# Sums of squares as two short passes instead of one full one: retention's variances and the scan's group norms

## The chip, the cores and the metric

The kernel runs on one core of a Trainium2 chip. The metric is the device time of one launch in microseconds. A core has five engines that run side by side and wait for each other through semaphores: TensorE (PE in profiles; PEld is its weight loading), VectorE (DVE), ScalarE (ACT), GpSimd (POOL) and SyncE (SP), which here only starts transfers. Each engine works through its own list in order.

## The reference

A three-part network on 512 positions of width 1024, in fp32: a first block with three mixers, a layer of retention and neighbourhood attention, a layer with a bidirectional state scan (SSD), and a gated feed-forward block behind each of the last two. Two places matter here. Both take a mean of squares over features and scale by its inverse root.

```python
# retention: 8 heads of 64, y already has its head's mean taken off
var = jnp.mean(jnp.square(y - mu), axis=-1, keepdims=True)
y = ((y - mu) * lax.rsqrt(var + EPS)) * ret_gn_g
...
# scan: 4 groups of 512 features
y = y + xh * d_skip                       # then gated by silu(z)
yg = y.reshape(bsz, s, SSD_GROUPS, SSD_INNER // SSD_GROUPS)
yg = yg * lax.rsqrt(jnp.mean(yg * yg, axis=-1, keepdims=True) + EPS)
```

## The kernel before

Activations lie with features on the 128 partitions and the 512 positions along the row; a tile is 128 x 512. Weights come in slots of 128 x 1024 through a ring of five buffers.

**Short and full products.** A weight matmul is done as three short products (type fp32r): ScalarE copies the operand to fp32r, the high part (`hi`); VectorE subtracts it from the operand, the low part (`lo`); TensorE adds high x high, high x low and low x high (L439 to L441). Matmuls with plain fp32 operands are full products; the trace shows each as two records. Sums over features are full products with a matrix of ones: `ones64` (ones within each head of 64) for retention, `ones` for the scan.

**Retention.** Four pairs of heads, p = 0 to 3, eight steps r = 2p, 2p+1. TensorE's list alternates scores, states and values of a pair with the tiles of `in2`. The sum of squares of pair p-1 (`ret_variance`) stands behind the tiles of step 2p; the last one stands in `out2_pe`, in front of the second k of `out2`'s lead (n == 1). Around it: VectorE copies y out of PSUM (`keep_ret`, L1390), ScalarE squares it (`square`, L1193), TensorE sums (L1073), ScalarE takes Ln and Exp (`roots`), VectorE refines and scales (`norm`).

**The scan.** Four groups g, each of eight heads and four output tiles. Per group the order in TensorE's list (`ssd_pe`) is: states and between-chunk products, mixed with tiles of `z`; then for i = 0 to 3 a set of four transposes that carry y into PSUM (`carried`, L2514) and the head products (`inside`, L2521). `carried(g, 0)` waits for `comb`, which VectorE's `carry(g, 2)` completes (L2799); `inside(g, i)` waits for `mlu`, the weighed matrices of heads 2i, 2i+1 (`weigh`, L2836). For the last group, out3's first products stand between them and wait for `ylo`, y's low parts (`low`, L2885).

The decay matrices of the heads come in pairs: SP loads two rows of `cum_rows` for each head (`load_rows`), and waits for the head two before to have been moved; ScalarE moves one to PSUM (`moved_back`, L2652), VectorE joins (`join`, L2826), ScalarE exponentiates (`decays`, L2662), VectorE weighs. In group g ScalarE's list runs: `squares(g-1, 2)`, moves of heads 0, 1, a weight split, `squares(g-1, 3)`, `decays(g, 0, 1)`, `moved_back(g, 2, 3)`, a weight split, `decays(g, 2, 3)`, and so on.

The sum of squares of group g-1 is spread over the engines. ScalarE squares the four tiles (L2626), GpSimd adds them up in three adds (L2759), TensorE sums over features (`norm_sum`, L2530; for the last group in `out3_lead_pe`, L2602). GpSimd's list in group g is written out by hand:

```python
        for g in range(SG):
            if g:
                pool.wait_ge(comb, 6 * g + 1)
                add_squares(pool, g - 1, 1)
                gate(pool, g - 1, 3)
                add_squares(pool, g - 1, 2)
            for d, (c, held) in enumerate(((2, 3), (1, 0))):
                pool.wait_ge(comb, 6 * g + 2 + d + 1)
                nc.gpsimd.tensor_tensor(y12[:, c, :], y12[:, c, :], y12[:, held, :], ALU.add).then_inc(y12_added, 1)
            if g:
                add_squares(pool, g - 1, 3)
```

`comb` 6g+3 and 6g+4 come from VectorE's `carry(g, 1)`. `norm_sum(g-1)` stands in front of `carried(g, 0)`, in the last group in front of `carried(g, 1)`; it waits for all three adds (`yadd`). Squares and sums are held in the rows of `xbc` that B and C of the group no longer need (`B_TILE + g`, `C_TILE + g`).

Of the kernel before, what the change touches and what calls it, by code (L numbers as in the profile page):

```python
# [185 lines left out]
def build(nc, dr, ctx, start):  # L186
# [110 lines left out]
    sq_2 = at("sq_2", [P, KT, S], ST + 64)  # L297
    nrm_2 = at("nrm_2", [P, 3, S], ST + 58)
    sq_u = at("sq_u", [P, KT, S], ST + 72)
    nrm_u = [at(f"nrm_u{i}", [P, S], ST + kb)[:, :] for i, kb in enumerate((96, 100, 98))]  # L300
    sq_x = at("sq_x", [P, KT, S], ST + 32)
    nrm_x = [at(f"nrm_x{i}", [P, S], ST + kb)[:, :] for i, kb in enumerate((88, 93, 90))]
# [573 lines left out]
    sign = nstat[:, 3, 0:1]  # L876
    rg, rh = sem("rg"), sem("rh")
    rz, ra, rv, ryc = sem("rz"), sem("ra"), sem("rv"), sem("ryc")
    g_sq, g_var, g_ln, g_norm, g_gate, g_last = (sem(n) for n in ("g_sq", "g_var", "g_ln", "g_norm", "g_gate", "g_last"))
    bt_load, bm_done, cm_load = [sem("bt_load0"), sem("bt_load1")], sem("bm_done"), sem("cm_load")  # L880
    (nvp, nvc, nz, ns, nmax, nexp, nrec, nnorm, ntp, ntc, ny, nyc) = (
        sem(n) for n in ("nvp", "nvc", "nz", "ns", "nmax", "nexp", "nrec", "nnorm", "ntp", "ntc", "ny", "nyc"))
# [186 lines left out]
        mm.then_inc(rv, 1)  # L1069

    def ret_variance(pe, p):
        pe.wait_ge(g_sq, p + 1)
        nc.tensor.matmul(bank[2 + p % 2][:, :], C["ones64"], gsq[:, :], start=True, stop=True).then_inc(g_var, 1)  # L1073

    def two_pe(pe):
        before, home = SUMS["in2"]
# [42 lines left out]
    def out2_pe(pe):  # L1119
        for n, k in enumerate(MIX2_ORDER):  # L1120
            pe.wait_ge(mixlo, KT + n + 1)
            if n == 1:
                ret_variance(pe, PAIRS - 1)
            for t in range(LEAD["out2"]):
                if n == 0:
                    bank_clear(pe, "out2", t)
                    pe.wait_ge(lo_done, last_slot("out2", t) + 1 + HEAD)
                mm = three("out2", t, k, a_hi, a_lo, S, n == KT - 1, MIX2_ORDER[0])
                if n == KT - 1:
                    mm.then_inc(slot_done, 1)  # L1130
# [136 lines left out]
    def two_dve(dve):  # L1267
# [183 lines left out]
        for r in range(RET_STEPS):  # L1451
            p, half = r // 2, r % 2
            if half:
                states(p)
                if p:
                    norm(p - 1)
            else:
                if p:
                    keep_ret(p - 1)
                weigh(p)  # L1460
                query_decay(p)
            if r < RET_STEPS - 1:
                for t in RET_TILES[r]:
                    tile(t)
# [1 line left out]
        take(27)  # L1466
        lo_to(dve, split_ahead("in2", 27))
        keep_ret(PAIRS - 1)
        for n in range(1, 4):
            low(n)  # L1470
        low(4)
        low(5)
        norm(PAIRS - 1)
# [728 lines left out]

    def one_pool(pool):
        pool.wait_ge(cst_load, 16)
        nc.gpsimd.tensor_copy(tri_r[:, 0, :], C["neg_tri"])
        nc.gpsimd.tensor_copy(tri_r[:, 1, :], C["neg_ones"]).then_inc(tri_ready, 1)
        tile_gone(pool, "in1", 1)
# [35 lines left out]
                mask(aw, n, a_done, ZU * p + n + 1, am_done)  # L2243


    (dtw_load, dtw_hi, dtw_lo, dtp, dtc, cump, cum_x, dt_ok, tri_load, y12_added, cs_rows) = (
        sem(n) for n in ("dtw_load", "dtw_hi", "dtw_lo", "dtp", "dtc", "cump", "cum_x", "dt_ok", "tri_load", "y12_added", "cs_rows"))
    xmid, xtap, xsilu, zs_done = sem("xmid"), sem("xtap"), sem("xsilu"), sem("zs_done")
    (tbp, tbc, gp, gl_done, txp, xtc, vt_done, stp, hub, hu, inter, comb) = (
        sem(n) for n in ("tbp", "tbc", "gp", "gl_done", "txp", "xtc", "vt_done", "stp", "hub", "hu", "inter", "comb"))  # L2250
# [50 lines left out]

    def cum_pe(pe):
        pe.wait_ge(dt_ok, 1)
        pe.wait_ge(tri_load, 16)
        tile_gone(pe, "xbc", 8)
        for half, (mf, mb) in enumerate((("gt", "lt"), ("le", "ge"))):
            out = bank[CUM_BANK][:, 256 * half:256 * (half + 1)].rearrange("p (c d h) -> p c d h", c=TT, d=2)
            nc.tensor.matmul(out[:, :, 0, :], M[mf], da[:, :, 0, :], start=True, stop=True)
            nc.tensor.matmul(out[:, :, 1, :], M[mb], da[:, :, 1, :], start=True, stop=True)
        nc.tensor.matmul(bank[TOTAL_BANK][:, 0:256], C["ones"], flat(da), start=True, stop=True).then_inc(cump, 1)  # L2310
        for c in range(TT):
            for d, m in enumerate(("le", "ge")):
                mm = nc.tensor.matmul(bank[CST_BANK][SH * d:SH * (d + 1), c * P:(c + 1) * P], da[:, c, d, :], M[m], start=True, stop=True)
        mm.then_inc(cump, 1)
# [51 lines left out]
    def cum_act(act):  # L2366
# [2 lines left out]
            nc.scalar.activation(flat(dst), source, ACT.Exp).then_inc(cum_x, 1)  # L2369
        nc.scalar.activation(flat(lndt), flat(lndt), ACT.Ln).then_inc(cum_x, 1)  # L2370
        act.wait_ge(cump, 2)
        act.wait_ge(tri_load, 16)
# [73 lines left out]
    def ssd_pe(pe):  # L2446
# [78 lines left out]
            mm.then_inc(intra, 1)  # L2525

        def norm_sum(g):
            pe.wait_ge(yadd, 3 * (g + 1))
            pe.wait_ge(hu, 4 * min(g + 2, SG))
            nc.tensor.matmul(bank[6][:, :], C["ones"], xbc[:, B_TILE + g, :], start=True, stop=True).then_inc(ysum, 1)  # L2530

        for t in range(2):
            for q in range(4):
# [10 lines left out]
        for g in range(SG):  # L2544
# [17 lines left out]
            for i in range(4):  # L2562
                first, second = (4 * g + 4 + i // 2, 2 * (i % 2)), (4 * g + 4 + i // 2, 2 * (i % 2) + 1)
                if i == 0 and not last:
                    part_z(*first)
                    part_z(*second)
                if g and i == last:
                    norm_sum(g - 1)
                carried(g, i)
                if i:  # L2570
# [15 lines left out]
    def out3_step(pe, t, k):  # L2586
# [6 lines left out]
        if k % 8 == 7:  # L2593
            mm.then_inc(slot_done, 1)

    def out3_lead_pe(pe):
        pe.wait_ge(joined, HEADS)
        for t in (2, 3):
            for k in range(8):
                out3_step(pe, t, k)  # L2600
        pe.wait_ge(yadd, 3 * SG)
        nc.tensor.matmul(bank[6][:, :], C["ones"], xbc[:, B_TILE + SG - 1, :], start=True, stop=True).then_inc(ysum, 1)  # L2602
        for t in range(4):
            for k in range(8, 12):
                out3_step(pe, t, k)
        for t in range(4):
            for k in range(12, XS_TILES):
                out3_step(pe, t, k)
        pe.wait_ge(yev, XS_TILES)
        for t in range(4, FULL["out3"]):  # L2610
            tile_pe(pe, "out3", t, y_hi, y_lo)
        out_tail_pe(pe, 2, y_hi, y_lo, sq_b, nrm_b[:, 0, :])
# [8 lines left out]
    def squares(g, i):  # L2621
# [3 lines left out]
            act_.wait_ge(yadd, 3 * g + 1)  # L2625
        nc.scalar.activation(square_home(g, i), xbc[:, k, :], ACT.Square).then_inc(ysq, 1)  # L2626

    def group_roots_act(g):
        act_.wait_ge(ysum, g + 1)
        nc.scalar.activation(xbc[:, C_TILE + g, :], bank[6][:, :], ACT.Ln, scale=1.0 / GW, bias=eps_col[:, :]).then_inc(yln, 1)  # L2630
        act_.wait_ge(yln, 2 * g + 1)
# [6 lines left out]
    def ssd_act(act):  # L2638
# [33 lines left out]
        for g in range(SG):  # L2672
# [18 lines left out]
            if g:  # L2691
                squares(g - 1, 3)
            decays(g, 0, 1)
            moved_back(g, 2, 3)
            hi_to(act, z0 + 4 * g + 7)
            decays(g, 2, 3)
# [64 lines left out]
    def ssd_dve(dve):  # L2761
# [76 lines left out]
        def evac_y(g, i):  # L2838
# [2 lines left out]
            nc.vector.scalar_tensor_tensor(out=xbc[:, k, :], in0=xbc[:, k, :], scalar=pcol("d_skip", k), in1=bank[2 + i % 2][:, :],  # L2841
                                           op0=ALU.mult, op1=ALU.add).then_inc(yev, 1)

        def root_first(g):
            dve.wait_ge(yln, 2 * g + 2)
# [43 lines left out]
        for g in range(SG):  # L2889
# [27 lines left out]
            else:  # L2917
                lo_to(dve, z0 + 4 * g + 5)
                carry(g, 2)
                weigh(g, 0, 1)  # L2920
            if last:
                low(0)
                low(1)
# [53 lines left out]
        lo_to(dve, z0 + 4 * SG + 4)  # L2977
        for k in range(9, 12):
            low(k)
        lo_to(dve, z0 + 4 * SG + 7)  # L2980
        group_roots(SG - 1)
        for i in range(4):
# [83 lines left out]
    def _(act):  # L3066
# [28 lines left out]
        up_act(act, 0)  # L3095
        nc.scalar.preload_act_table_set(LOGEXP)
        act.wait_ge(glo, FT)
        act.dma_start(wdt[:, :, :], dr["w_dt"]).then_inc(dtw_load, 16)
        act.wait_ge(dtw_load, 16)
# [3 lines left out]
        act.dma_start(tri[:, :, :], dr["tri"]).then_inc(tri_load, 16)  # L3103
        hi_to(act, PLAN["xbc"]["slot0"] + 5)
        xbc_act(act)
        turned_x(act, 0, 2)
# [201 lines left out]
```

## Time and profile before

| | |
|---|---|
| median of 3 executions | 1658.52 us (1658.38 to 1660.28) |
| profiled execution | 1660.08 us, its span 1658.3 us |
| TensorE busy | 1643.7 us, 99% of the span |
| VectorE, ScalarE, GpSimd busy | 1160.1, 797.2, 210.7 us |

The span runs from the first to the last instruction. Times in a timeline are microseconds from its start; a matmul's end is modelled, so the distance between starts tells more of TensorE than a duration. The scan takes from about 1035 to 1205 us, retention from about 370 to 482 us. Idle time is shown in brackets with what ended it.

### The profile page before, as it was taken

To read this page: it belongs to the slowest core of one execution; us is meant where nothing else is said; L and a number is where in the kernel's file an instruction comes from. 1 tells how busy PE (TensorE), PEld (TensorE's weight loads), DVE (VectorE), ACT (ScalarE), POOL (GpSimd) and SP (SyncE) were. 2 spreads that over 40 slices of the span, in tenths; PEclk is the share of its full clock that TensorE was granted. 3 is DMA by queue.
4 is the path that set the end of the run, shared out by engine and by line. 5 is a ranking of instruction groups with operands and counts; after the bars stand their busy time and mean duration, and the time that the engine had idled before them with its cause. 6 is when DMAs were issued, how large, how long until landed. Compare 5 with 4: busy or idle time off the path is not lost.

```text
span 1658.3 us, 21247 instructions
## 1 busy us (share of the span) xinstructions
PE 1643.7 (99%) x8278; PEld 1335.5 (81%) x8278; DVE 1160.1 (70%) x1681; ACT 797.2 (48%) x1367; POOL 210.7 (13%) x244
## 2 busy tenths in 40 slices
PE   9999999999999999999999999999999999999998
PEld 6877878788888888888888888777688888888887
DVE  5585874985668887664238999799984788666324
ACT  5475753552254554443224455777853554444221
POOL 0442100442110011110000000122200011111000
PEclk9999999999999999999999999999999999999999
DMA  6211223234332232333332224555333223233332
GB/s 236 91 64 63 77 77 126 93 92 86 77 102 69 97 102 91 101 97 103 93 96 83 94 92 123 153 153 149 106 102 112 71 97 102 90 101 94 97 92 73
DMA packets 55108, 166.53 MB, mean 100 GB/s; under 512 B 6816, under 2 KB 10144, under 8 KB 54880
## 3 DMA queue, kind: packets, MB, share of 16 engines
q1 hardware_dynamic: 51024, 158.80, 30.5%
q0 software_dynamic: 1536, 2.10, 1.2%
q10 hardware_dynamic: 2448, 4.27, 0.8%
q8 instruction: 66, 1.08, 0.3%
q14 instruction: 34, 0.28, 0.1%
HBM read 160.82 MB, written 2.23 MB: 98 GB/s over the span
## 4 chain that ended last, share of the span: by engine, by line
PE 91%; DVE 6%; ACT 2%; DMA 1%; issue 1%; ACTq 0%; DVEq 0%; SPq 0%
PE bank L439 25%; PE bank L441 25%; PE bank L440 25%; PE bank L456 2%; PE bank L457 2%; PE bank L458 2%; PE bank L2493 1%; DVE cv L2427 1%; PE bank L2505 1%; PE bank L2521 1%; DVE a_lo L813 1%; DVE w_lo L402 1%; ACT a_hi L776 1%; DVE x L707 1%; PE bank L1619 1%
## 5 line engine op out<-in xcount | busy, mean ns | idle before, releaser
L439 PE MATMUL bank<-a_hi,w_hi 128*128 128x512 f32 x1384 | 556.4, 402 | 2.5 <-DVE a_lo L595 1.8
L402 DVE TENSOR_TENSOR w_lo<-raw,w_hi 128x1024 fp32r<-128x1024 f32 (+1 forms) x257 | 327.5, 1280 | 329.8 <-ACT w_hi L395 329.0
L441 PE MATMUL bank<-a_hi,w_lo 128*128 128x512 f32 x1384 | 539.5, 390 | 0.0
L440 PE MATMUL bank<-a_lo,w_hi 128*128 128x512 f32 x1384 | 538.9, 389 | 0.0
L395 ACT ACTIVATE w_hi<-raw 128x1024 fp32r<-128x1024 f32 (+1 forms) x259 | 267.9, 1041 | 316.4 <-DMA raw<-in_w_down 141.5
L439 PEld LDWEIGHTS bank<-a_hi,w_hi 128*128 128x128 f32 x1384 | 259.9, 188 | 68.0 <-issue 13.2
L440 PEld LDWEIGHTS bank<-a_lo,w_hi 128*128 128x128 f32 x1384 | 260.0, 188 | 59.4 <-issue 7.4
L441 PEld LDWEIGHTS bank<-a_hi,w_lo 128*128 128x128 f32 x1384 | 259.8, 188 | 55.2
L1500 ACT ACTIVATE u<-bank,par 128x512 f32<-128x512 f32 x88 | 68.5, 779 | 176.0 <-DVE bank L864 176.0
L1543 POOL TENSOR_TENSOR gv<-u 128x512 f32<-128x512 f32 x44 | 57.4, 1304 | 577.1 <-DVE u L1519 577.1
L441 PE MATMUL bank<-g_hi,w_lo 128*128 128x512 f32 x308 | 119.8, 389 | 0.0
L439 PE MATMUL bank<-g_hi,w_hi 128*128 128x512 f32 x308 | 119.8, 389 | 0.0
L440 PE MATMUL bank<-g_lo,w_hi 128*128 128x512 f32 x308 | 119.8, 389 | 0.0
L2427 DVE SCALAR_TENSOR_TENSOR cv<-bank,par,cv 128x510 f32<-128x510 f32 (+1 forms) x96 | 71.7, 748 | 2.5
L1519 DVE SCALAR_TENSOR_TENSOR u<-bank,par,u 128x511 f32<-128x511 f32 x88 | 66.0, 750 | 3.1
L439 PEld LDWEIGHTS bank<-g_hi,w_hi 128*128 128x128 f32 x308 | 57.8, 188 | 12.1
L440 PEld LDWEIGHTS bank<-g_lo,w_hi 128*128 128x128 f32 x308 | 57.8, 188 | 12.1
L441 PEld LDWEIGHTS bank<-g_hi,w_lo 128*128 128x128 f32 x308 | 57.8, 188 | 11.9
L1516 DVE SCALAR_TENSOR_TENSOR u<-bank,par,u 128x511 f32<-128x511 f32 x88 | 65.0, 739 | 0.0
L864 DVE TENSOR_TENSOR bank<-bank,nrm_u 128x512 f32<-128x512 f32 x88 | 60.8, 690 | 0.8 <-PE bank L441 0.8
L456 PE MATMUL bank<-a_hi,w_hi 128*128 128x256 f32 (+1 forms) x156 | 49.9, 320 | 2.4 <-DVE a_lo L813 1.2
L2742 POOL TENSOR_TENSOR y<-y 128x512 f32<-128x512 f32 x8 | 10.1, 1287 | 303.6 <-DVE y L2799 303.6
(429 smaller groups left out, 2478.8 us busy)
## 6 DMA issues: line engine op xcount, KB each, us to landing
raw<-in_w_up SPq DMA_DIRECT2D x86, 512.0 KB, 3.6
raw<-in_w_in SPq DMA_DIRECT2D x50, 512.0 KB, 3.7
raw<-in_w_out SPq DMA_DIRECT2D x32, 512.0 KB, 3.7
raw<-in_w_down SPq DMA_DIRECT2D x32, 512.0 KB, 3.5
raw<-in_w_xbc SPq DMA_DIRECT2D x23, 512.0 KB, 3.6
back<-cum_rows SPq DMA_DIRECT2D x32, 256.0 KB, 4.2
em<-cum_rows SPq DMA_DIRECT2D x32, 256.0 KB, 5.3
raw<-in_w_z SPq DMA_DIRECT2D x16, 512.0 KB, 4.5
```

The source lines that it names most:

```text
L395: nc.scalar.activation(hi_of(q)[:, 0:w], raw_of(q)[:, 0:w], ACT.Copy).then_inc(hi_done, 1)
L402: nc.vector.tensor_tensor(lo_of(q)[:, 0:w], raw_of(q)[:, 0:w], hi_of(q)[:, 0:w].bitcast(F32), ALU.subtract).then_inc(lo_done, 1)
L439: nc.tensor.matmul(out, wh, rhs_hi[:, k, :], start=k == first, stop=False)
L440: nc.tensor.matmul(out, wh, rhs_lo[:, k, :], start=False, stop=False)
L441: return nc.tensor.matmul(out, wl, rhs_hi[:, k, :], start=False, stop=stop)
L456: nc.tensor.matmul(out, wh, rhs_hi[:, k, cols], start=start, stop=False, skip_group_check=True)
L864: nc.vector.tensor_tensor(tile_bank(name, t)[:, :], tile_bank(name, t)[:, :], r, ALU.mult).then_inc(scaled, 1)
L1500: nc.scalar.activation(u[:, t % 4, :], tile_bank(name, t)[:, :], ACT.Identity, scale=pcol(f"ffn_w{layer}", 3 * t + 1), bias=pcol(f"ffn_b{l ...
L1516: nc.vector.scalar_tensor_tensor(out=ut[:, 1:S], in0=pt_[:, 0:S - 1], scalar=pcol(w, 3 * t), in1=ut[:, 1:S], op0=ALU.mult, op1=ALU.add).th ...
L1519: nc.vector.scalar_tensor_tensor(out=ut[:, 0:S - 1], in0=pt_[:, 1:S], scalar=pcol(w, 3 * t + 2), in1=ut[:, 0:S - 1], op0=ALU.mult, op1=ALU ...
L1543: nc.gpsimd.tensor_tensor(gv[:, i % 2, :], u[:, 2 * i % 4, :], u[:, 2 * i % 4 + 1, :], ALU.mult).then_inc(prod, 1)
L2427: nc.vector.scalar_tensor_tensor(out=dst, in0=tile_bank("xbc", tile)[:, a + by:b + by], scalar=pcol("conv_w", 5 * tile + tap), in1=dst, op ...
```

## The change

Each of the eight sums becomes two short products with a copy of the ones in fp32r: one over the high part of the squares, one over the low part, added in the same PSUM bank.

- GpSimd makes the fp32r copies of `ones` and `ones64` at the start.
- Retention: ScalarE's `square` gets a second step, the high copy (into `gsq_parts`); VectorE gets `square_low`, behind `query_decay` in steps 2, 4, 6, and for the last pair between `low(2)` and `low(3)`. TensorE waits for `g_low`. The last sum moves from n == 1 to n == 2.
- Scan: ScalarE gets `group_high_act(g-1)` between `decays(g, 0, 1)` and `moved_back(g, 2, 3)`; it waits for the third add. VectorE gets `group_low(g-1)` behind `weigh(g, 0, 1)` (in the last group behind the weight split that follows them). TensorE's sum waits for `sum_low` and moves one i later: in front of `carried(g, 1)` in groups 1 and 2, of `carried(g, 2)` in group 3. For the last sum the two new steps stand behind `high(11)` and `low(11)`, and the products behind the first four of out3's middle steps.
- Two load semaphores are merged into one (`scan_load`).

```diff
@@ buffers
+    ones_r = at("ones_r", [P, P], 103, F32R)
+    ones64_r = at("ones64_r", [P, P], 102, F32R)
+    gsq_parts = at("gsq_parts", [P, 2, S], ST + 76, F32R)
+    xbc_r = at("xbc_r", [P, 24, S], ST + 32, F32R)
@@ ret_variance
-        pe.wait_ge(g_sq, p + 1)
-        nc.tensor.matmul(bank[2 + p % 2][:, :], C["ones64"], gsq[:, :], start=True, stop=True).then_inc(g_var, 1)
+        pe.wait_ge(g_low, p + 1)
+        nc.tensor.matmul(bank[2 + p % 2][:, :], ones64_r[:, :], gsq_parts[:, 0, :], start=True, stop=False)
+        nc.tensor.matmul(bank[2 + p % 2][:, :], ones64_r[:, :], gsq_parts[:, 1, :], start=False, stop=True).then_inc(g_var, 1)
@@ out2_pe
-            if n == 1:
+            if n == 2:
                 ret_variance(pe, PAIRS - 1)
@@ two_act, square
             nc.scalar.activation(gsq[:, :], p2[:, RET_V + p, :], ACT.Square).then_inc(g_sq, 1)
+            act.wait_ge(g_sq, 2 * p + 1)
+            nc.scalar.activation(gsq_parts[:, 0, :], gsq[:, :], ACT.Copy).then_inc(g_sq, 1)
@@ two_dve
+        def square_low(p):
+            dve.wait_ge(g_sq, 2 * p + 2)
+            nc.vector.tensor_tensor(gsq_parts[:, 1, :], gsq[:, :], gsq_parts[:, 0, :].bitcast(F32), ALU.subtract).then_inc(g_low, 1)
...
                 query_decay(p)
+                if p:
+                    square_low(p - 1)
...
-        for n in range(1, 4):
+        for n in range(1, 3):
             low(n)
+        square_low(PAIRS - 1)
+        low(3)
@@ one_pool
+        nc.gpsimd.tensor_copy(ones_r[:, :], C["ones"])
+        nc.gpsimd.tensor_copy(ones64_r[:, :], C["ones64"])
@@ ssd_pe
         def norm_sum(g):
-            pe.wait_ge(yadd, 3 * (g + 1))
             pe.wait_ge(hu, 4 * min(g + 2, SG))
-            nc.tensor.matmul(bank[6][:, :], C["ones"], xbc[:, B_TILE + g, :], start=True, stop=True).then_inc(ysum, 1)
+            group_sum(pe, g)
...
-                if g and i == last:
+                if g and i == 1 + last:
                     norm_sum(g - 1)
@@ new, and out3_lead_pe
+    def group_sum(pe, g):
+        pe.wait_ge(sum_low, g + 1)
+        nc.tensor.matmul(bank[6][:, :], ones_r[:, :], xbc_r[:, C_TILE + g, :], start=True, stop=False)
+        nc.tensor.matmul(bank[6][:, :], ones_r[:, :], xbc_r[:, B_TILE + g, :], start=False, stop=True).then_inc(ysum, 1)
...
-        pe.wait_ge(yadd, 3 * SG)
-        nc.tensor.matmul(bank[6][:, :], C["ones"], xbc[:, B_TILE + SG - 1, :], start=True, stop=True).then_inc(ysum, 1)
         for t in range(4):
             for k in range(8, 12):
                 out3_step(pe, t, k)
+            if t == 0:
+                group_sum(pe, SG - 1)
@@ ssd_act
+    def group_high_act(g):
+        act_.wait_ge(yadd, 3 * (g + 1))
+        nc.scalar.activation(xbc_r[:, C_TILE + g, :], xbc[:, B_TILE + g, :], ACT.Copy).then_inc(yln, 1)
...
             decays(g, 0, 1)
+            if g:
+                group_high_act(g - 1)
             moved_back(g, 2, 3)
...
             high(4 * SG - 8 + i)
+        group_high_act(SG - 1)
@@ ssd_dve
+        def group_low(g):
+            dve.wait_ge(yln, 3 * g + 1)
+            nc.vector.tensor_tensor(xbc_r[:, B_TILE + g, :], xbc[:, B_TILE + g, :], xbc_r[:, C_TILE + g, :].bitcast(F32), ALU.subtract).then_inc(sum_low, 1)
...
                 carry(g, 2)
                 weigh(g, 0, 1)
+            if g:
+                group_low(g - 1)
...
             low(k)
+        group_low(SG - 1)
         lo_to(dve, z0 + 4 * SG + 7)
```

## Rows read from the trace of the kernel before

**Rows 1.** The page, busy time of each engine.
```profile
PE 1643.7 (99%) x8278; PEld 1335.5 (81%) x8278; DVE 1160.1 (70%) x1681; ACT 797.2 (48%) x1367; POOL 210.7 (13%) x244
```

**Rows 2.** The chain, one retention sum: start us, us, what.
```profile
409.26 0.86 PE bank L1073 x2
410.12 0.23 PE bank L439
```

**Rows 3.** Timeline of TensorE behind head products: start us, us, what.
```profile
1118.16 0.50 PE L439 MATMUL bank<-a_hi,w_hi 128*128 128x512 f32 x1
1118.49 0.39 PE L440 MATMUL bank<-a_lo,w_hi 128*128 128x512 f32 x1
```

**Rows 4.** Timeline of ScalarE, retention's first square.
```profile
406.45 0.61 ACT L1193 ACTIVATE gsq<-p 128x512 f32<-128x512 f32 x1
```

**Rows 5.** TensorE's waits, 1040 to 1240 us: total, times, longest.
```profile
PE bank L2514 <- DVE y L2799: 1.3, 1, 1.3
PE bank L2480 <- DVE xtok L2805: 0.3, 1, 0.3
```

**Rows 6.** Windows: PE, PEld, DVE, ACT, POOL busy, granted clock, DMA, GB/s.
```profile
1163.00:1183.00 20.00, 19.99 (x72) 12.89 (x73) 19.88 (x29) 15.56 (x39) 8.54 (x8) 1.00 0.47 111
```

**Rows 7.** Timeline of ScalarE in groups 1 and 3.
```profile
1088.59 2.45 ACT L2662 ACTIVATE em<-em,lbias 128x128 f32<-128x128 f32 x8 [0.63 <-DVE em L2826]
1090.95 2.40 ACT L2652 ACTIVATE bank<-back,between_bias 128x128 f32<-128x128 f32 x8
...
1109.05 2.57 ACT L2652 ACTIVATE bank<-back,between_bias 128x128 f32<-128x128 f32 x8 [3.85 <-DMA em<-cum_rows]
...
1175.12 2.44 ACT L2662 ACTIVATE em<-em,lbias 128x128 f32<-128x128 f32 x8
```

**Rows 8.** Timeline of GpSimd: the third add in groups 1 and 3.
```profile
1095.86 1.27 POOL L2759 TENSOR_TENSOR xbc<-xbc 128x512 f32<-128x512 f32 x1
...
1182.46 1.28 POOL L2759 TENSOR_TENSOR xbc<-xbc 128x512 f32<-128x512 f32 x1
```

**Rows 9.** Timeline of VectorE in groups 1 and 3 and behind them.
```profile
1095.39 1.36 DVE L2826 COPY_PREDICATED em<-later,bank 128x512 f32<-128x512 int32 x2
...
1098.14 1.28 DVE L2799 TENSOR_TENSOR y<-bank,cume 128x512 f32<-128x512 f32 x2
...
1199.14 0.69 DVE L2836 TENSOR_TENSOR em<-em,gmat 128x512 f32<-128x512 f32 x1 [0.22 <-ACT em L2662]
...
1225.07 2.49 DVE L2885 TENSOR_TENSOR y_lo<-xbc,y_hi 128x512 fp32r<-128x512 f32 x4
```

**Rows 10.** Timeline of TensorE in groups 1 and 3 and behind them.
```profile
1100.45 1.02 PE L2530 MATMUL bank<-xbc,cst 128*128 128x512 f32 x2
...
1102.86 0.66 PE L2514 MATMUL bank<-cst,y 128*128 128x128 f32 x4
...
1185.54 0.66 PE L2514 MATMUL bank<-cst,y 128*128 128x128 f32 x4 [1.28 <-DVE y L2799]
...
1187.16 1.12 PE L2530 MATMUL bank<-xbc,cst 128*128 128x512 f32 x2
1188.13 0.60 PE L2514 MATMUL bank<-cst,y 128*128 128x128 f32 x4
1188.48 0.48 PE L439 MATMUL bank<-y_hi,w_hi 128*128 128x512 f32 x1
...
1200.17 1.09 PE L2521 MATMUL bank<-em,xtok 128*64 128x128 f32 x16
...
1226.71 0.39 PE L439 MATMUL bank<-y_hi,w_hi 128*128 128x512 f32 x1
```

**Rows 11.** Timeline of SP's queue: a row load of group 1.
```profile
1103.38 0.43 SPq L2995 DMA_DIRECT2D em<-cum_rows  x1
```

**Rows 12.** The core's span and its mean granted TensorE clock.
```profile
core 0: 1658.3 us, clock 1.000
```

**Rows 13.** Full products at the start: ns min/median/max, first and last start.
```profile
L690 PE MATMUL bank<-spin x8: 592/752/1219, 1.4 to 6.2; 128*128 128x512 f32 x8
```

More of the change, by code:

```diff
@@ L878, in build @@
     rz, ra, rv, ryc = sem("rz"), sem("ra"), sem("rv"), sem("ryc")
-    g_sq, g_var, g_ln, g_norm, g_gate, g_last = (sem(n) for n in ("g_sq", "g_var", "g_ln", "g_norm", "g_gate", "g_last"))
+    g_sq, g_low, g_var, g_ln, g_norm, g_gate, g_last = (sem(n) for n in ("g_sq", "g_low", "g_var", "g_ln", "g_norm", "g_gate", "g_last"))
     bt_load, bm_done, cm_load = [sem("bt_load0"), sem("bt_load1")], sem("bm_done"), sem("cm_load")
@@ L2243, in one_pool @@
                 mask(aw, n, a_done, ZU * p + n + 1, am_done)
-    (dtw_load, dtw_hi, dtw_lo, dtp, dtc, cump, cum_x, dt_ok, tri_load, y12_added, cs_rows) = (
-        sem(n) for n in ("dtw_load", "dtw_hi", "dtw_lo", "dtp", "dtc", "cump", "cum_x", "dt_ok", "tri_load", "y12_added", "cs_rows"))
+    (scan_load, dtw_hi, dtw_lo, dtp, dtc, cump, cum_x, dt_ok, y12_added, cs_rows) = (
+        sem(n) for n in ("scan_load", "dtw_hi", "dtw_lo", "dtp", "dtc", "cump", "cum_x", "dt_ok", "y12_added", "cs_rows"))
     xmid, xtap, xsilu, zs_done = sem("xmid"), sem("xtap"), sem("xsilu"), sem("zs_done")
@@ L2303, in cum_pe @@
         pe.wait_ge(dt_ok, 1)
-        pe.wait_ge(tri_load, 16)
+        pe.wait_ge(scan_load, 32)
         tile_gone(pe, "xbc", 8)
@@ L2371, in cum_act @@
         act.wait_ge(cump, 2)
-        act.wait_ge(tri_load, 16)
+        act.wait_ge(scan_load, 32)
         nc.scalar.activation(later[:, :], M["gt"], ACT.Copy)
@@ L2626, in squares @@
         nc.scalar.activation(square_home(g, i), xbc[:, k, :], ACT.Square).then_inc(ysq, 1)
+    sum_low = sem("sum_low")
+    def group_high_act(g):
+        act_.wait_ge(yadd, 3 * (g + 1))
+        nc.scalar.activation(xbc_r[:, C_TILE + g, :], xbc[:, B_TILE + g, :], ACT.Copy).then_inc(yln, 1)
     def group_roots_act(g):
@@ L2630, in group_roots_act @@
         nc.scalar.activation(xbc[:, C_TILE + g, :], bank[6][:, :], ACT.Ln, scale=1.0 / GW, bias=eps_col[:, :]).then_inc(yln, 1)
-        act_.wait_ge(yln, 2 * g + 1)
+        act_.wait_ge(yln, 3 * g + 2)
         nc.scalar.activation(xbc[:, B_TILE + g, :], xbc[:, C_TILE + g, :], ACT.Exp, scale=-0.5).then_inc(yln, 1)
@@ L2842, in evac_y @@
                                            op0=ALU.mult, op1=ALU.add).then_inc(yev, 1)
+        def group_low(g):
+            dve.wait_ge(yln, 3 * g + 1)
+            nc.vector.tensor_tensor(xbc_r[:, B_TILE + g, :], xbc[:, B_TILE + g, :], xbc_r[:, C_TILE + g, :].bitcast(F32), ALU.subtract).then_inc(sum_low, 1)
         def root_first(g):
[L2845 removed]
+            dve.wait_ge(yln, 3 * g + 3)
             nc.vector.scalar_tensor_tensor(out=xbc[:, C_TILE + g, :], in0=bank[6][:, :], scalar=GW * EPS, in1=xbc[:, B_TILE + g, :],
@@ L3097, in _ @@
         act.wait_ge(glo, FT)
-        act.dma_start(wdt[:, :, :], dr["w_dt"]).then_inc(dtw_load, 16)
-        act.wait_ge(dtw_load, 16)
+        act.dma_start(wdt[:, :, :], dr["w_dt"]).then_inc(scan_load, 16)
+        act.wait_ge(scan_load, 16)
         nc.scalar.activation(wdt_hi[:, :, :], wdt[:, :, :], ACT.Copy).then_inc(dtw_hi, 1)
@@ L3102, in _ @@
         boundary_act(act, 1, EV_POST1, rows(nrm_b), sq_b, "mix_pre1", sq_x, "xbc", EV_XBC, nrm_x)
-        act.dma_start(tri[:, :, :], dr["tri"]).then_inc(tri_load, 16)
+        act.dma_start(tri[:, :, :], dr["tri"]).then_inc(scan_load, 16)
         hi_to(act, PLAN["xbc"]["slot0"] + 5)
```

## The prediction

> **What bounds the kernel now.** I read the page's busy table first: TensorE is busy for 99% of the span [rows 1]. So time is removed by taking work off TensorE, and added by every wait put in front of it. The change does both. So I went on to the chain and the timeline of TensorE around old sums, then to the timelines of the other engines in the scan, where the new steps are put. That stage has only two TensorE waits now, 1.3 us and 0.3 us [rows 5], but the cover behind them is thin: VectorE is busy 19.9 of 20 us in one of its stretches [rows 6].
>
> **The change: TensorE's work.** One old sum is a full-precision product in two records. The chain gives it 0.86 us, and 0.23 us to a short product behind it [rows 2]. Two short products are 0.46 us, so each of retention's four sums gives 0.40 us, 1.6 us together, if the operands are there. In the scan the sums of groups 0, 1 and 2 stand behind head products (L2521) afterwards. A short product behind those takes 0.33 us instead of 0.23 [rows 3], so there the new sum is 0.56. The first two give 0.30 us each; group 2's took 0.97 (1187.16 to 1188.13) [rows 10] and gives 0.41; the last, behind short products, 0.40. All eight: 1.6 + 0.6 + 0.41 + 0.40 = 3.0 us, 0.18% of the time. That is the most that the change can bring.
>
> **Retention: operands in time.** ScalarE's square ends at 407.06 [rows 4]; a copy behind it costs the same 0.61 us, the subtraction on VectorE about 0.68 (its other copies and products of this size): ready at 408.4, and TensorE comes at 409.26 [rows 2]. The second and third have about as much. VectorE waits 1.1 us in front of a weight split that would have run. Cover: that slot's weights are read a tile or more later. The fourth sum is moved one k back (twelve short products, 2.7 us), and its low part is ready about 0.5 us before it. I cost these at nothing; without the cover it would be up to 0.7 us each (the subtraction). POOL's two small copies of ones stand ahead of all its work at the start, where TensorE doesn't wait for it, and the renamed load semaphore adds no wait: both nothing.
>
> **The scan: the copy that waits.** The new copy of group g-1's sum (its high part) stands on ScalarE between the exponentials of heads 0, 1 and the moves of heads 2, 3 of group g, and it waits for the third add of squares. That add is the last thing in GpSimd's sequence: it comes behind two additions on y that wait for VectorE's second carry. In group 1 it ends at 1095.86 + 1.27 = 1097.13 [rows 8], while ScalarE had its exponentials done at 1091.04 and started the moves right behind them [rows 7]. ScalarE works in order, so all that is behind the copy waits some 6 us. Worked on for group 1:
> - copy at 1097.17, moves from 1097.7 at 1.2 us a head: done 1098.95 and 1100.15.
> - VectorE's joins of heads 2, 3 ran at 1095.39 to 1096.75 [rows 9]; the second now ends at 1100.9. Behind them in order come a weight split and the last carries, 2.67 us to 1099.42 in the rows, less 0.35 that GpSimd's add cost the split there: carries done at 1103.22, and heads 0, 1 weighed 1.2 later.
> - TensorE, with the old sum gone, is there at 1100.45. It waits to 1103.28 for the carries, runs four transposes, waits to 1104.5 for the weighed heads, then 1.03 for the head products and 0.56 for the sum. Its next transposes start at 1106.1, and they started at 1102.86 [rows 10]: 3.2 us lost.
> - Late next: the moves of heads 2, 3 release SP's row loads for heads 4, 5, which take 5.7 us to ScalarE's start (1103.38 to 1109.05) [rows 7, 11], and then those for 6, 7. Carried through in the same way, heads 6, 7 are weighed at 1119.4, and TensorE wants them at 1120.6: nothing more.
>
> Group 2 repeats the pattern (three groups show it), 0.2 us worse: 3.4. TensorE's 0.3 us wait for xtok behind it, and 0.1 beside it, go, since VectorE is then less late than TensorE: -0.4.
>
> Group 3: the add ends at 1183.74, the moves are done at 1185.54 and 1186.72, the joins at 1187.39, one weighing and the carries at 1189.27. TensorE starts its transposes at 1189.33 where it was 1185.54 (+3.8). It loses the old sum (+2.8), but its first out3 product needs y_lo: a weighing, a weight split, the new subtraction and one y_lo end at 1192.2, so it starts at 1192.25 against 1188.48 (+3.8). The new sum adds 0.56 (+4.3). Two row loads in turn put the moves of heads 6, 7 at 1201.8, their exponentials at 1204.9, the weighing at 1205.65: the last head products, at 1200.17 before, start at 1205.7 (+5.5). There VectorE had 0.3 us in hand (1199.14 + 0.69) [rows 9, 10].
>
> From there VectorE runs without a pause. The first of the last four y_lo ended 0.96 us ahead of its product (1225.07 + 0.68 against 1226.71) [rows 9, 10]; it is 0.34 later against TensorE, TensorE comes 0.40 earlier, and the new subtraction adds 0.6. So the 0.40 of the last sum is given back.
>
> **Sum.** -1.6 + 3.2 + 3.4 - 0.4 + 5.5 = +10.1 us. The profiled execution had a span of 1658.3 in 1660.08; the median is 1658.52, and since what lies around the span doesn't change I add it there: **1668.6 us**. Bounds: at least, group 3 loses no more than group 1, and every wait is 0.4 shorter by overlap: 3 x 2.8 - 0.4 - 1.6 = +6.4. At most, the row loads take a quarter more (1.4 us each, two in turn), of which 1.2 is in hand: 1.6 more a group, +14.9.
>
> **Rivals.**
> - *The wait is covered* (the other side). ScalarE's moves were ready 2.0 us ahead of the joins (1093.35, 1095.39), VectorE's carries 1.0 ahead of TensorE without its sum (1099.42, 1100.45), and 0.35 of GpSimd's disturbance goes: 3.4 us. If the third add ended no more than that after ScalarE's exponentials, all 3.0 us would be kept: 1655.5. It ends 6.1 us after them in group 1 and 6.2 in group 3 (1183.74, 1177.56) [rows 7, 8]. For it speaks that ScalarE is idle half the time [rows 1].
> - *One group pays.* VectorE and GpSimd work ahead after the first wait, so only group 3, where a wait stands already, pays: 5.5 - 3.0 = +2.5, 1661.0. Against it: the carry that starts GpSimd's adds hangs on TensorE's own state products, so the add can't come earlier against TensorE.
> - *TensorE slows after the waits.* Its waits in the scan are at most 1.3 us now [rows 5], and the mean granted clock is 1.000 (2.4 GHz) [rows 12]. My waits are 2.8, 3.0 and 5.1 us, longer than any there. At the program's start single records of the same full product take up to 1219 ns against 592 [rows 13], so twice as long is the bound. Twice the 1.5 us behind group 3's wait and the 1.4 of a pair of out3 steps add 2.9, less 1.0 that the y_lo wait hides, and some 1 in the other groups: +3, 1671.6. The Trainium skill ("TensorE: Matmul & The Clock Gate", Part 1) says that the clock of an idle TensorE is throttled to half; no stretch of this trace tests it.
>
> **Chances.** Forecast 0.70, slower clock 0.12, covered 0.08, one group 0.10. Range: the forecast's own bounds (1664.9 to 1673.4) with the slower clock and part of one group beside them: 1663.0 to 1675.0. A measurement here tells about 0.2% (3.3 us) from no change. Covered is split, since 3.0 us lies just inside that bound (faster 0.03, same 0.05); one group is mostly same (+0.15%): 0.06, the rest slower. Faster 0.03, same 0.11, slower 0.86.
>
> **What would show it.** On ScalarE in groups 1 to 3, an idle stretch of about 6 us in front of the new copy, released by GpSimd's add. VectorE's joins of heads 2, 3 some 4 us later against its own states. TensorE waits of 2.8 to 5.1 us at the first transposes behind the states, for VectorE's y. In retention no new wait on TensorE, and 0.40 us less a sum. If the copy doesn't wait, or the joins come at their old place, the forecast is wrong, and 1655.5 is the number. Wrong in size only: row loads faster or slower than 5.7 us, or a granted clock below 1.00.

## The result, and the profile after

The changed kernel takes **1672.6 us** (median of 6, 1671.02 to 1674.48) against 1659.42 for the kernel before (median of 6, 1658.38 to 1660.28): a ratio of 1.0079, with a 95% interval from 1.0069 to 1.0089. Forecast were 1668.6 (1663.0 to 1675.0) and slower with a chance of 0.86. The change costs 13.2 us and the forecast said 10.1. Trace against trace it is 12.2 us (spans 1658.3 and 1670.5).

The page of the changed kernel, busy time of each engine. It answers to [rows 1].

```profile
PE 1647.3 (99%) x8278; PEld 1340.0 (80%) x8278; DVE 1162.5 (70%) x1689; ACT 801.6 (48%) x1375; POOL 215.0 (13%) x246
```

TensorE's busy time was to fall by the 3.0 us of the sums and it rose by 3.6. So two things need an explanation: longer waits, and products that take longer. The waits of TensorE in the same stretch as [rows 5]: total, times, longest.

```profile
PE bank L2531 <- DVE y L2829: 10.2, 3, 4.8
PE bank L2538 <- DVE em L2866: 0.5, 1, 0.5
```

One wait of 1.3 us has become three of 10.2 together. The wait for xtok (0.3) is gone. Next ScalarE in group 1, which answers to [rows 7], and GpSimd's third add, which answers to [rows 8].

```profile
1086.73 2.45 ACT L2689 ACTIVATE em<-em,lbias 128x128 f32<-128x128 f32 x8 [0.62 <-DVE em L2856]
1095.29 0.63 ACT L2653 ACTIVATE xbc_r<-xbc 128x512 fp32r<-128x512 f32 x1 [6.11 <-POOL xbc L2789]
1095.82 2.40 ACT L2679 ACTIVATE bank<-back,between_bias 128x128 f32<-128x128 f32 x8
```

```profile
1093.98 1.27 POOL L2789 TENSOR_TENSOR xbc<-xbc 128x512 f32<-128x512 f32 x1
```

The copy (L2653) waits 6.11 us for the add, and the moves of heads 2, 3 (L2679) stand behind it. Before, they ran right behind the exponentials. Groups 2 and 3 show 6.21 and 6.11. VectorE behind it, in group 1, which answers to [rows 9]:

```profile
1097.08 0.75 DVE L2856 COPY_PREDICATED em<-later,bank 128x512 f32<-128x512 int32 x1 [3.48 <-ACT bank L2679]
1098.26 0.74 DVE L2856 COPY_PREDICATED em<-later,bank 128x512 f32<-128x512 int32 x1 [0.42 <-ACT bank L2679]
1098.89 1.21 DVE L406 TENSOR_TENSOR w_lo<-raw,w_hi 128x1024 fp32r<-128x1024 f32 x1
1100.02 1.28 DVE L2829 TENSOR_TENSOR y<-bank,cume 128x512 f32<-128x512 f32 x2
```

VectorE is idle for 3.48 us in front of the joins, where it had none [rows 6, 9], and its last carries end at 1101.3. TensorE's first transposes start there. TensorE in groups 1, 2 and 3, which answers to [rows 10]:

```profile
1101.35 1.12 PE L2531 MATMUL bank<-cst,y 128*128 128x128 f32 x4 [2.60 <-DVE y L2829]
1102.55 1.97 PE L2538 MATMUL bank<-em,xtok 128*64 128x128 f32 x16
1104.45 0.50 PE L2614 MATMUL bank<-xbc_r,ones_r 128*128 128x512 f32 x1
...
1105.02 0.60 PE L2531 MATMUL bank<-cst,y 128*128 128x128 f32 x4
...
1148.33 0.71 PE L2531 MATMUL bank<-cst,y 128*128 128x128 f32 x4 [2.77 <-DVE y L2829]
...
1153.73 0.63 PE L444 MATMUL bank<-a_lo,w_hi 128*128 128x512 f32 x1
1154.16 0.63 PE L445 MATMUL bank<-a_hi,w_lo 128*128 128x512 f32 x1
...
1156.00 0.40 PE L444 MATMUL bank<-a_lo,w_hi 128*128 128x512 f32 x1
...
1196.57 1.11 PE L2531 MATMUL bank<-cst,y 128*128 128x128 f32 x4 [4.81 <-DVE y L2829]
...
1212.29 1.09 PE L2538 MATMUL bank<-em,xtok 128*64 128x128 f32 x16
```

Behind each wait the products are slow. The head products (x16) take 1.97 us and not 1.09. In group 2 short products follow each other at 0.43 us (1153.73, 1154.16) up to 1155.4, then at 0.23 again. The windows around the waits show why. Each row has the window and its length, then the busy time of PE, PEld, DVE, ACT and POOL, then the granted clock, the DMA share and GB/s.

```profile
1101.00:1105.00 4.00, 3.57 (x22) 2.72 (x23) 3.95 (x7) 1.79 (x6) 0.00 (x0) 0.57 0.91 264
1105.00:1110.00 5.00, 5.00 (x38) 4.03 (x37) 3.26 (x5) 4.64 (x14) 0.00 (x0) 1.00 0.75 194
1148.00:1156.00 8.00, 7.18 (x34) 5.70 (x34) 5.66 (x10) 4.65 (x14) 0.00 (x0) 0.57 0.59 189
...
1196.50:1200.00 3.50, 3.43 (x22) 2.77 (x23) 3.50 (x7) 2.97 (x9) 0.00 (x0) 0.51 0.92 299
```

The granted clock is 0.57, 0.57 and 0.51 there, which is near its lower level (1.2 GHz), and 1.00 (2.4 GHz) in the window behind the first (and in those behind the others). A table of TensorE's starts, the kernel before against the changed one, adds up where the 12.2 us came from. Each difference is that of the same instruction in the two timelines (before, changed), less what stood in the rows above.

| stretch | measured | forecast |
|---|---|---|
| up to the last states of group 1 (1095.97, 1094.11) | -1.86 | -1.6 |
| group 1, to the second transposes (1102.86, 1105.02) | +4.02 | +3.2 |
| group 2, to the third transposes (1150.14, 1158.27) | +6.09 | +3.4 |
| between the groups (xtok's wait and others; last states of group 3 at 1182.39, 1189.88) | -0.76 | -0.4 |
| group 3, to the last head products (1200.17, 1212.29) | +4.63 | +5.5 |
| from there to the end | +0.05 | 0 |

In retention the sums are as forecast. TensorE at the first of them, which answers to [rows 2]:

```profile
408.77 0.39 PE L1077 MATMUL bank<-gsq_parts,ones_r 128*128 128x512 f32 x1
409.00 0.39 PE L1078 MATMUL bank<-gsq_parts,ones_r 128*128 128x512 f32 x1
409.23 0.39 PE L443 MATMUL bank<-a_hi,w_hi 128*128 128x512 f32 x1
```

From the sum to the next product it is 0.46 us (408.77 to 409.23) where it was 0.86. VectorE's low part starts at 407.46 and takes 0.69, so it ends 0.6 us ahead of the first of the two products.

### The profile page after: what moved, and what is told of

It is laid out like the page before. It is cut to its first block, busy times and chain, and to the rows that moved or that the text cites. A ratio compares the mean times of both kernels' runs of the same rounds, so it can differ in the third digit from the quotient of the medians.

```text
span 1670.5 us, 21265 instructions
## 1 busy us (share of the span) xinstructions
PE 1647.3 (99%) x8278; PEld 1340.0 (80%) x8278; DVE 1162.5 (70%) x1689; ACT 801.6 (48%) x1375; POOL 215.0 (13%) x246
## 4 chain that ended last, share of the span: by engine, by line
PE 87%; DVE 7%; ACT 2%; DMA 2%; issue 1%; POOL 1%; ACTq 0%; DVEq 0%; SPq 0%
PE bank L443 24%; PE bank L445 24%; PE bank L444 24%; PE bank L460 2%; PE bank L461 2%; PE bank L462 2%; DVE cv L2444 1%; DVE w_lo L406 1%; PE bank L2538 1%; DVE a_lo L817 1%; ACT bank L2679 1%; ACT a_hi L780 1%; DVE x L711 1%; PE bank L1634 1%; PE bank L1666 1%
## 5 line engine op out<-in xcount | busy, mean ns | idle before, releaser
L399 ACT ACTIVATE w_hi<-raw 128x1024 fp32r<-128x1024 f32 (+1 forms) x259 | 267.8, 1040 | 319.1 <-DMA raw<-in_w_down 142.1
L443 PEld LDWEIGHTS bank<-a_hi,w_hi 128*128 128x128 f32 x1384 | 260.2, 188 | 67.2 <-issue 12.2
L444 PEld LDWEIGHTS bank<-g_lo,w_hi 128*128 128x128 f32 x308 | 57.8, 188 | 12.1
L445 PEld LDWEIGHTS bank<-g_hi,w_lo 128*128 128x128 f32 x308 | 57.8, 188 | 12.1
L2772 POOL TENSOR_TENSOR y<-y 128x512 f32<-128x512 f32 x8 | 10.1, 1283 | 304.0 <-DVE y L2829 304.0
```

Of the source, the lines that this page charges most:

```text
L399: nc.scalar.activation(hi_of(q)[:, 0:w], raw_of(q)[:, 0:w], ACT.Copy).then_inc(hi_done, 1)
L443: nc.tensor.matmul(out, wh, rhs_hi[:, k, :], start=k == first, stop=False)
L444: nc.tensor.matmul(out, wh, rhs_lo[:, k, :], start=False, stop=False)
L445: return nc.tensor.matmul(out, wl, rhs_hi[:, k, :], start=False, stop=stop)
```

## The experiments

Each is timed beside the kernel before (1659.33 us for the first four, 21 runs; 1659.17 for the last three, 27 runs).

### The third add ahead of y's additions

```diff
@@ ssd_pool
                 gate(pool, g - 1, 3)
                 add_squares(pool, g - 1, 2)
+                add_squares(pool, g - 1, 3)
             for d, (c, held) in enumerate(((2, 3), (1, 0))):
...
-            if g:
-                add_squares(pool, g - 1, 3)
```

> The changed kernel with one move in GpSimd's sequence: the third add of squares right behind the second, ahead of the two additions on y. Theory (ScalarE's new copy waits for an add that stands behind VectorE's second carry): the copy finds its operand ready, the 6 us idle stretches on ScalarE and TensorE's waits of 2.6 to 4.8 us go, and with them the slow clock; what stays is the saving of the short passes, so 2 to 3 us below the kernel before: about 1657. Rival (the added copy and subtraction, 0.6 us each on engines that have almost no time in hand, are what costs): at or above 1662, with TensorE's waits still there.

Measured: 1657.98 us (1657.47 to 1658.62, 11 runs), ratio 0.9993, interval 0.9984 to 1.0001. So 14.6 us of the changed kernel's time go with the place of one add. TensorE's waits in the scan:

```profile
PE bank L2531 <- DVE y L2828: 1.6, 1, 1.6
PE bank L443 <- DVE y_lo L2918: 0.7, 1, 0.7
PE bank L443 <- issue: 0.3, 1, 0.3
```

The three long waits are gone and the granted clock is 1.000. But of the 3.0 us that the short sums could bring (the expectation said 2 to 3), 1.35 arrive. A new wait for y_lo stands in group 3. VectorE and TensorE there:

```profile
1184.35 0.69 DVE L2875 TENSOR_TENSOR xbc_r<-xbc,xbc_r 128x512 fp32r<-128x512 f32 x1
1184.95 1.29 DVE L2918 TENSOR_TENSOR y_lo<-xbc,y_hi 128x512 fp32r<-128x512 f32 x2
```

```profile
1184.37 0.66 PE L2531 MATMUL bank<-cst,y 128*128 128x128 f32 x4
1185.69 0.50 PE L443 MATMUL bank<-y_hi,w_hi 128*128 128x512 f32 x1 [0.66 <-DVE y_lo L2918]
...
1186.94 0.47 PE L443 MATMUL bank<-y_hi,w_hi 128*128 128x512 f32 x1 [0.27 <-issue]
```

The new subtraction (L2875) stands right in front of y_lo, and TensorE, without the old sum in that place, comes early and waits.

### Only retention's sums short

The scan is put back as in the kernel before; retention is as in the changed one.

```diff
@@ group_sum, put back
-        pe.wait_ge(sum_low, g + 1)
-        nc.tensor.matmul(bank[6][:, :], ones_r[:, :], xbc_r[:, C_TILE + g, :], start=True, stop=False)
-        nc.tensor.matmul(bank[6][:, :], ones_r[:, :], xbc_r[:, B_TILE + g, :], start=False, stop=True).then_inc(ysum, 1)
+        pe.wait_ge(yadd, 3 * (g + 1))
+        nc.tensor.matmul(bank[6][:, :], C["ones"], xbc[:, B_TILE + g, :], start=True, stop=True).then_inc(ysum, 1)
...
-            if g:
-                group_high_act(g - 1)
...
-            if g:
-                group_low(g - 1)
```

> Only retention's four sums in two short passes; the scan's four as in the kernel before. Theory: the part costs nothing on the other engines, so 0.40 us a sum, 1.6 us below the kernel before (1657.8), and the scan as before with its waits of 1.3 and 0.3 us. Rival (VectorE's wait in front of a weight split is paid for later): no gain or a loss of up to 3 us, with a new wait of TensorE in 400 to 480 us.

Measured: 1657.47 us (1656.87 to 1659.02, 11 runs), ratio 0.9991, interval 0.9982 to 1.0000: 1.9 us less than before, where the term was 1.6. The whole of the loss lies in the scan. Against the first experiment it is 0.5 us faster (medians; resampling the runs of the two gives 0.1 to 1.0), so the four short sums of the scan brought nothing even with the early add.

### The wait alone

```diff
@@ ssd_act of the kernel before
             decays(g, 0, 1)
+            if g:
+                act.wait_ge(yadd, 3 * g)
             moved_back(g, 2, 3)
```

> The kernel before with one line added: ScalarE waits for the third add between the exponentials of heads 0, 1 and the moves of heads 2, 3. No short passes, no new copies. Theory (the wait is the cause): as slow as the changed kernel or slower, since nothing is saved: 1672 to 1676, with TensorE waiting for VectorE's y in groups 1 to 3 and a granted clock under 1.00 behind those waits. Rival (the new work is the cause): within 2 us of the kernel before.

Measured: 1671.39 us (1670.8 to 1671.79, 4 runs), ratio 1.0074, interval 1.0061 to 1.0088: +12.1 us with no copy, no subtraction and all sums as before. ScalarE in group 1, and TensorE's waits in the scan:

```profile
1096.67 2.42 ACT L2652 ACTIVATE bank<-back,between_bias 128x128 f32<-128x128 f32 x8 [6.11 <-POOL xbc L2761]
```

```profile
PE bank L2514 <- DVE y L2801: 7.0, 3, 4.3
PE bank L2480 <- DVE xtok L2807: 1.3, 1, 1.3
PE bank L2521 <- DVE em L2838: 1.1, 2, 0.5
```

The same 6.11 us on ScalarE. The wait alone brings most of the loss, but not all of it: 1672 us or more was expected. The changed kernel's scan loses 15.1 us (13.2 and the 1.9 that retention gains), this one 12.1. TensorE in groups 1 and 2:

```profile
1102.23 0.66 PE L2514 MATMUL bank<-cst,y 128*128 128x128 f32 x4 [1.24 <-DVE y L2801]
...
1148.89 0.66 PE L2514 MATMUL bank<-cst,y 128*128 128x128 f32 x4 [1.43 <-DVE y L2801]
```

Here the old sum still stands in front of the first transposes and fills 0.86 us of each wait; the changed kernel has its sum behind them. From the last states to the second transposes of group 1 it is 9.09 us here and 10.91 in the changed kernel, to the third transposes of group 2 it is 13.56 and 17.35. Part of this comes back behind them, where this run waits 1.3 us for xtok and the changed kernel doesn't. So the sum's later place, and the lower clock that the changed kernel has in group 2 and this run hasn't, seem to add to the loss; no run tests the place alone.

### TensorE kept busy through the waits

In the changed kernel 12 short products of ones with ones (20 in group 3), whose result nobody uses, stand in front of the transposes.

```diff
@@ ssd_pe
+                if g and i == 0:
+                    for _ in range(20 if last else 12):
+                        nc.tensor.matmul(bank[7][:, :].rearrange("p (r c) -> p r c", r=4), ones_r[:, :], ones_r[:, :].unsqueeze(1).to_broadcast([P, 4, P]), start=True, stop=True)
```

> The changed kernel, with idle products put in front of the first transposes of groups 1 to 3 (12, 12 and 20 short ones into a bank that nobody reads), so that TensorE works where it would wait. The output doesn't change. Theory (the clock falls because TensorE idles, and costs some 3 to 4 us of the 13): the waits for VectorE's y stay the same length for all that is behind them, the granted clock stays 1.00, and the time is 3 to 4 us below the changed kernel: about 1669. Rival (the products behind the wait are slow for another reason, or are hidden by VectorE anyway): within 1 us of the changed kernel, 1672 to 1673.

Measured: 1670.19 us (1669.82 to 1670.37, 4 runs), ratio 1.0067, interval 1.0054 to 1.0081: 2.4 us less than the changed kernel, for more work, where 3 to 4 were expected. TensorE in groups 1 and 2, and the window of group 2:

```profile
1099.16 2.88 PE L2585 MATMUL bank<-ones_r 128*128 128x512 f32 x12
1101.95 0.66 PE L2531 MATMUL bank<-cst,y 128*128 128x128 f32 x4
1103.15 1.09 PE L2538 MATMUL bank<-em,xtok 128*64 128x128 f32 x16 [0.54 <-DVE em L2869]
```

```profile
1148.00:1156.00 8.00, 7.37 (x59) 5.42 (x58) 7.01 (x13) 6.12 (x20) 0.00 (x0) 1.00 0.75 233
```

The granted clock stays at 1.00 in all three groups and the head products take 1.09 us again. In group 2, from the states to the third transposes, it is 14.55 us (1141.38 to 1155.93) against 17.35 in the changed kernel (1140.92 to 1158.27): the clock's price there is 2.8 us. In group 1, from the last states to the second transposes, it is 10.07 us (1094.68 to 1104.75) against 10.91 (1094.11 to 1105.02): 0.84 us. In group 3, from the last states to the last head products, nothing is won: 22.57 us (1187.95 to 1210.52) against 22.41 (1189.88 to 1212.29), since TensorE then waits 0.66 us for y_lo. Of the 3.6 us of the first two groups, 1.1 goes between the groups, 0.3 of it in a wait for xtok, and this execution was 0.6 us later at group 1.

### Group 2's sum full again

The first experiment with the sum that falls into group 3 a full product at its old place, without its copy and its subtraction.

```diff
+    SHORT = (0, 1, 3)
...
     def group_sum(pe, g):
+        if g not in SHORT:
+            pe.wait_ge(yadd, 3 * (g + 1))
+            nc.tensor.matmul(bank[6][:, :], C["ones"], xbc[:, B_TILE + g, :], start=True, stop=True).then_inc(ysum, 1)
+            return
...
-                if g and i == 1 + last:
+                if g and i == (1 + last if g - 1 in SHORT else last):
```

> The third add early, as in the first experiment, and the sum of group 2 (the one that falls into group 3) a full product again at its old place, with no copy on ScalarE and no subtraction on VectorE there; the other seven sums short. Theory (in group 3 the new subtraction stands ahead of y_lo, for which out3's first product waits, and costs more than the short passes save): the first transposes of group 3 still wait some 1.3 us as in the kernel before, the wait for y_lo is gone, group 3 takes no longer than before, and the time is 1656.5 to 1657.2, some 1 us under the first experiment's 1657.98. Rival (the loss in group 3 comes from VectorE's order in general and not from that sum's steps): it stays at 1657.8 to 1658.3.

Measured: 1657.35 us (1656.85 to 1658.37, 11 runs), ratio 0.9990, interval 0.9981 to 0.9999. TensorE in group 3:

```profile
1182.45 0.66 PE L2531 MATMUL bank<-cst,y 128*128 128x128 f32 x4 [1.22 <-DVE y L2837]
...
1184.07 1.12 PE L2618 MATMUL bank<-xbc,cst 128*128 128x512 f32 x2
1185.03 0.60 PE L2531 MATMUL bank<-cst,y 128*128 128x128 f32 x4
1185.39 0.47 PE L443 MATMUL bank<-y_hi,w_hi 128*128 128x512 f32 x1
...
1197.04 1.09 PE L2538 MATMUL bank<-em,xtok 128*64 128x128 f32 x16
```

The wait for y_lo is gone. From the first transposes to the last head products it is 14.59 us (1182.45 to 1197.04), in the first experiment 15.66 (1182.75 to 1198.41), in the kernel before 14.63 [rows 10]. In both runs the first out3 product starts 2.94 us behind the first transposes (1182.45 to 1185.39, 1182.75 to 1185.69). So taking the full product of 0.97 us out of that place brought nothing: TensorE waited for y_lo instead, which stands behind the new subtraction. Behind it the first experiment loses 0.57 us more among out3's products and 0.50 us by the short sum at its new place: 1.07 us. In the medians 0.63 us of it is seen, 0.47 if each is taken against the kernel before beside it; the runs of the two overlap, and 1657.35 lies between the expectation's 1657.2 and the rival's 1657.8. It is the traces that speak for the subtraction.

### The last sum full too

```diff
+    SHORT = (0, 1)
```

> As the run before it, with the last sum (group 3's own, in out3's lead) a full product at its old place too; short: retention's four and the sums of groups 0 and 1. The prediction's step (the last sum's 0.40 us is given back to y_lo behind it): within 0.1 us of the run before, or 0.2 faster. Rival (the 0.40 is kept): 0.4 us slower than the run before.

Measured: 1657.31 us (1656.72 to 1658.54, 11 runs), ratio 0.9988, interval 0.9979 to 0.9997. The medians show no difference between the last sum short and full (1657.35, 1657.31), but with this spread they can't exclude 0.4 us. The traces say the same: from the last head products to the end of the span it is 458.1 us in the kernel before and 458.2 in this run (full), 458.1 in the first experiment and 458.6 in the run before this one (short). In the first experiment the next product starts 0.47 us behind the second one of the sum (1216.14, 1216.61), and short products otherwise follow at 0.23; the profile names no releaser for it. So part of the 0.40 is gone right behind the sum and not at the y_lo named in the prediction. It is the fastest median, but its lead over retention alone (0.16 us) is nothing that these runs can tell.

### The copy behind the exponentials of heads 2, 3

The changed kernel with GpSimd's order untouched.

```diff
@@ ssd_act
             decays(g, 0, 1)
-            if g:
-                group_high_act(g - 1)
             moved_back(g, 2, 3)
             hi_to(act, z0 + 4 * g + 7)
             decays(g, 2, 3)
+            if g:
+                group_high_act(g - 1)
```

> The changed kernel with GpSimd's order untouched and ScalarE's copy moved behind the exponentials of heads 2, 3 of the group, so that the moves of heads 2, 3 no longer stand behind it. Theory (the loss comes from what stands behind the waiting copy on ScalarE): the copy waits little or nothing, no TensorE wait above 1.7 us, granted clock 1.000, and the time is that of the first experiment within 1.5 us: 1657.5 to 1659.5. Rival (the late add itself is the cost, since TensorE's sum and VectorE's subtraction hang on it): 1662 or more, with TensorE waiting at the sum.

Measured: 1657.98 us (1657.41 to 1658.82, 11 runs), ratio 0.9993, interval 0.9984 to 1.0001, the time of the first experiment. ScalarE and GpSimd in group 1:

```profile
1094.58 2.46 ACT L2689 ACTIVATE em<-em,lbias 128x128 f32<-128x128 f32 x8 [1.83 <-DVE em L2856]
1096.94 0.62 ACT L2653 ACTIVATE xbc_r<-xbc 128x512 fp32r<-128x512 f32 x1
```

```profile
1094.29 1.28 POOL L2789 TENSOR_TENSOR xbc<-xbc 128x512 f32<-128x512 f32 x1
```

The add ends at 1095.57, as late as in the changed kernel (1095.25), and the copy doesn't wait for it, since its turn comes at 1096.94. TensorE waits 1.1 us for y and 0.7 for y_lo in group 3, much as in the first experiment, and nowhere in groups 1 and 2. So the late add is no cost; what stood behind the copy was.

## Why the prediction was right, and where its sizes were off

- **The mechanism** holds at each step that was named: 6.1 to 6.2 us idle on ScalarE in front of the copy, released by GpSimd's add; joins 3.5 us late; three waits of TensorE at the first transposes, 2.60, 2.77 and 4.81 us where 2.8, 3.0 and 5.1 were forecast. Three runs tell it from the others: the wait alone brings 12.1 us, and the loss goes whether the add is moved forward or the copy back. The total is nearer than its parts: groups 1 and 2 were 3.5 us too low, group 3 and the stretches between 1.2 too high.
- **Retention**: -1.9 measured alone, -1.6 forecast, no new wait in front of a sum. Each sum gives the 0.40; the rest is within what the runs tell.
- **Group 1** (+4.02, forecast 3.2) and **group 2** (+6.09, forecast 3.4). The step that was too small is the one that priced the work behind the waits at full clock, in the forecast's sum. In group 1 the head products took 1.90 us up to the sum (1102.55 to 1104.45) where 1.03 was set in: +0.87, the whole difference. In group 2 it was 2.8 us, and 6.09 - 2.8 = 3.3. The slower clock stood on record as a rival of 0.12 with +3 us for all groups; its 1671.6 is nearer to the measured 1672.6 than the forecast's 1668.6. But it put 1.9 of the 3 into group 3 and 1 into the others, and it came out the other way: 0.84 and 2.8 in groups 1 and 2, nothing in group 3 (22.57 against 22.41 with TensorE kept busy). It was no rival: it came on top of the forecast, and its chance should have been much higher, since the forecast itself held three waits longer than any of the scan's before.
- **Group 3** (+4.63, forecast 5.5). Here the step on the row loads failed: "Two row loads in turn put the moves of heads 6, 7 at 1201.8", and TensorE waiting for the weighed heads. It never waited there. ScalarE's moves in group 3 of the changed kernel, heads 5, 6 and 7:

```profile
1200.51 1.25 ACT L2679 ACTIVATE bank<-back,between_bias 128x128 f32<-128x128 f32 x4 [1.04 <-DMA em<-cum_rows]
...
1205.08 1.23 ACT L2679 ACTIVATE bank<-back,between_bias 128x128 f32<-128x128 f32 x4
...
1206.77 1.23 ACT L2679 ACTIVATE bank<-back,between_bias 128x128 f32<-128x128 f32 x4
```

  The moves of heads 6, 7 began at 1205.08 and 1206.77, with no idle time of ScalarE ahead of them, only 1.04 us once ahead of head 5's. The second ended at 1207.95; less the 7.49 us by which the trace was late at the start of group 3, that is 1200.5, 1.3 us ahead of the forecast (whose 1201.8 is their end, since its exponentials end at 1204.9). The last row load went out late:

```profile
1202.15 0.43 SPq L3032 DMA_DIRECT2D em<-cum_rows  x1
```

  It had landed when ScalarE came to it, so it took at most 4.6 us where 5.7 was set in. The last weighed head was there at 1211.6, 0.7 us ahead of TensorE. What was left is the forecast's +4.3 and 0.3 more.
- **The last sum** gave nothing, as said: tail +0.05. That its 0.40 us goes at the last four y_lo is not shown.
- **The rival of the covered wait** had the right condition (an early add) and a wrong price: 1655.5 with all 3.0 us kept. The early add gave 1657.98, and against the kernel before beside it 1.35 us and not 3.0. The traces of the first experiment and of retention alone name three places. The last sum's 0.40 was given back in the forecast itself but not by this rival. In group 3 the 0.41 forecast became a loss of 1.07. And the 0.7 us gained in groups 1 and 2 (63.30 us against 63.99 from the last states of group 1 to the last head products of group 2) went into the wait for y in group 3 that was there already: the first transposes start at 1182.75 in one and 1182.73 in the other. These traces lie 1.0 us apart where the medians lie 0.5, so the three are more than what is missing in the medians.
- **The rival of one group** is out: all three groups paid. Its price was also summed wrongly: the +5.5 of group 3 holds that group's sum and the last one already, so 2.2 and not 3.0 had to be taken off (+3.3, 1661.8).
- **Left open**: that exact splitting of the tenths, and how much of the loss is due to the sum's later place. The runs of one kernel spread over 1.1 to 2.2 us, and each trace is of one execution.

## What to carry to other kernels

A new step on an engine that works in order is priced by what stands behind it, and first by when its operand is there: here a copy of 0.6 us, put 6 us ahead of its operand, made the kernel 14.6 us slower than the same copy behind the next exponentials (1672.6 against 1657.98). Removing work from the busiest engine gains only where nothing else ends at that moment: a product taken away in front of an operand that isn't there yet turns into a wait. And when a forecast holds waits longer than any in the trace of before, the work behind them should be priced at both clocks.

## What the runs showed of the hardware

TensorE's granted clock fell close to its lower level (0.57, 0.57, 0.51) behind waits of 2.60, 2.77 and 4.81 us, and the work behind each was slow at first: 1.97 us for head products of 1.09. In groups 1 and 3 this was over some 3 us past the wait's end, in group 2 only at 1155.4, 7 us past it. Behind waits of 1.1 to 1.6 us in group 3 of the kernel before and of five experiments the head products took 1.09. With the wait alone, group 1 and group 2 of one execution differ: waits of 1.24 and 0.54 us close together were followed by a lower clock in group 1, waits of 1.43 and 0.54 in group 2 were not. The windows of that kernel:

```profile
1105.00:1110.00 5.00, 5.00 (x28) 3.95 (x28) 2.59 (x5) 3.60 (x11) 0.00 (x0) 0.73 0.98 209
1148.00:1156.00 8.00, 6.56 (x57) 5.17 (x57) 6.51 (x11) 6.06 (x19) 0.00 (x0) 1.00 0.81 233
```

So the length of a wait alone doesn't tell what the clock does behind it. The Trainium skill ("TensorE: Matmul & The Clock Gate", Part 1) says that an idle TensorE is throttled to half speed and that activity releases it. This case's traces agree: 0.57, 0.57 and 0.51 behind the waits, 1.00 when products that nobody uses fill them.
